# Two-layer hybrid decoder step: both halves of the next key pages turned at the head of a round, and gate halves dealt out to other rounds

## The reference

```python
gb, gc, hv, q, k, v, fl = jnp.split(h, splits, axis=-1)       # h = rmsnorm(x) @ w_in
yc, new_hist = causal_dwconv(gc * hv, hist, conv_w)           # 3 taps
y_a = gb * yc
...
s = jnp.einsum('bqhd,bkhd->bhqk', q, k) * (HEAD_DIM ** -0.5)  # 8 heads of 64
s = s + (cq[..., None] - ck[..., None, :])                    # sums of log forgets
p = jax.nn.softmax(jnp.where(k_pos <= q_pos, s, -inf), axis=-1)
out = jnp.einsum('bhqk,bkhd->bqhd', p, v)
...
k_all = jnp.concatenate([k_pool[page_table].reshape(bsz, p_len, h, d), k_new], axis=1)
```

## Time and profile before

| | us |
|---|---|
| median of 3 runs | 1504.37 |
| lowest, highest of them | 1501.26, 3993.2 |
| the profiled execution | 1502.65 |
| its span, first to last instruction | 1500.9 |
| TensorE busy in the span | 1409.4 (94%) |
| VectorE busy in the span | 721.5 (48%) |
| mean granted TensorE clock | 0.977 of full |

### The profile page before, as it was taken

The page is one execution under the profiler, slowest core; times in us unless marked ns, Lnnn a source line. Parts: engine busy times, 40 slices in busy tenths (PEclk is TensorE's granted clock), DMA queues, the critical chain, the costliest instruction groups (busy, mean ns, idle before and its releaser), DMA issues. The chain is left out here.

```text
span 1500.9 us, 34670 instructions
## 1 busy us (share of the span) xinstructions
PE 1409.4 (94%) x14005; PEld 1306.7 (87%) x14005; DVE 721.5 (48%) x1256; ACT 479.6 (32%) x706; POOL 594.9 (40%) x329
## 2 busy tenths in 40 slices
PE   7997888878799999999999999998999999999998
PEld 6895666666799999999999987875999999999998
DVE  5655678776444544203443366667455440044411
ACT  5474232233133222312223332116434422122221
POOL 2322222222233555444554454430445554455441
PEclk9998899998999999999999999998999999999999
DMA  5417679896632322333322446660423223323122
GB/s 180 127 52 237 230 262 319 302 336 200 213 88 67 97 84 73 92 102 91 92 63 62 134 125 163 153 167 2 124 62 93 84 67 101 113 82 87 52 80 74
DMA packets 246246, 192.56 MB, mean 128 GB/s; under 512 B 12129, under 2 KB 205106, under 8 KB 246058
## 3 DMA queue, kind: packets, MB, share of 16 engines
q1 hardware_dynamic: 244561, 188.31, 41.3%
q10 hardware_dynamic: 1181, 1.44, 0.4%
q0 software_dynamic: 400, 1.32, 0.3%
HBM read 173.03 MB, written 6.04 MB: 119 GB/s over the span
## 5 line engine op out<-in xcount | busy, mean ns | idle before, releaser
L683 POOL TENSOR_TENSOR w_l<-w_raw,w_h 128x1024 fp32r<-128x1024 f32 (+2 forms) x195 | 439.6, 2256 | 417.8 <-ACT w_h L830 397.0
L1804 PE MATMUL banks<-xa_h,w_h 128*128 128x272 f32 x1856 | 388.0, 290 | 4.4 <-DVE tmp L1627 3.3
L1804 PE MATMUL banks<-xa_h,w_l 128*128 128x272 f32 x1856 | 384.8, 289 | 0.0
L1804 PE MATMUL banks<-xa_l,w_h 128*128 128x272 f32 x1856 | 383.5, 288 | 0.0
L1804 PEld LDWEIGHTS banks<-xa_h,w_h 128*128 128x128 f32 x1856 | 293.2, 189 | 6.7 <-issue 5.4
L1804 PEld LDWEIGHTS banks<-xa_l,w_h 128*128 128x128 f32 x1856 | 292.4, 189 | 0.0
L1804 PEld LDWEIGHTS banks<-xa_h,w_l 128*128 128x128 f32 x1856 | 290.6, 189 | 0.0
L830 ACT ACTIVATE w_h<-w_raw 128x1024 fp32r<-128x1024 f32 (+2 forms) x193 | 185.1, 961 | 199.9 <-PE banks L1804 199.6
L1804 PE MATMUL banks<-h_h,w_h 128*128 128x272 f32 x928 | 192.7, 289 | 0.3 <-DVE x L1566 0.3
L1804 PE MATMUL banks<-h_h,w_l 128*128 128x272 f32 x928 | 192.3, 289 | 0.0
L1804 PE MATMUL banks<-h_l,w_h 128*128 128x272 f32 x928 | 191.6, 288 | 0.0
(11 more groups left out here) (302 smaller groups left out, 1682.3 us busy)
## 6 DMA issues: line engine op xcount, KB each, us to landing
w_raw<-in_w_up SPq DMA_DIRECT2D x88, 512.0 KB, 3.7
k_grp<-in_cache_k SPq DMA_DIRECT2D x128, 256.0 KB, 4.1
v_pg<-in_cache_v SPq DMA_DIRECT2D x120, 256.0 KB, 5.0
w_raw<-in_w_in SPq DMA_DIRECT2D x24, 512.0 KB, 6.0
w_raw<-in_w_down SPq DMA_DIRECT2D x32, 384.0 KB, 3.1
w_raw<-in_w_pw SPq DMA_DIRECT2D x24, 512.0 KB, 3.8
w_raw<-in_w_down SPq DMA_DIRECT2D x32, 320.0 KB, 3.0
w_raw<-in_w_out SPq DMA_DIRECT2D x8, 512.0 KB, 6.8
```

The source lines that it names most:

```text
L683: g.tensor_tensor(w_l[:, slot, 0:n], w_raw[:, slot, 0:n], w_h[:, slot, 0:n].bitcast(F32), ALU.subtract).then_inc(s_lo, 1)
L1804: ins = mm(out[:, half, 0:HT], w, v[:, half * HT:(half + 1) * HT], start=first and t == 0 and n == 0, stop=last and t == phase.tiles - 1 a ...
```

## The change

Two things change, the table of gate halves and the order of VectorE's program in a round.

```diff
 def gate_halves():
-    out = {0: ((0,), ()), 2: ((1,), (2,)), 3: ((3,), (4,)), 4: ((5,), (6,)), 16: ((18,), (19,)), 17: ((20,), (21,)),
+    out = {0: ((0,), ()), 2: ((1,), (2,)), 3: ((3,), (4,)), 4: ((5,), (6,)), 5: ((7,), ()), 6: ((8,), (9,)), 7: ((10,), ()), 8: ((11,), (12,)), 17: ((20,), (21,)),
            18: ((22,), (23,))}
-    for n in range(5, 16):
-        out[n] = ((n + 2,), ())
+    for n in range(9, 16):
+        out[n] = ((n + 4,), ())
...
                 if more:
                     key_turned(n + 1, 0)
+                    key_turned(n + 1, 1)
...
                 if n < PAIRS:
                     bias(2 * n)
                     bias(2 * n + 1)
+                    block_inverse(2 * n)
+                    block_inverse(2 * n + 1)
                 for q in halves_in(n):
                     half_scaled(q)
+                    if n < 17:
+                        gate_out(q)
+                if valued is not None and n >= 17:
+                    values(valued)
+                for q in halves_in(n) if n >= 17 else ():
                     gate_out(q)
-                if n < PAIRS:
-                    block_inverse(2 * n)
-                    block_inverse(2 * n + 1)
-                if more:
-                    key_turned(n + 1, 1)
                 if spread is not None:
                     total(spread)
...
-                if valued is not None:
+                if valued is not None and n < 17:
                     values(valued)
```

## The result

The changed kernel takes 1495.15 us in the median of its runs (1491.22 to 1501.35) against 1505.1 of the kernel before in the same session: a ratio of 0.9939, 95% interval 0.992 to 0.9959. It is faster by 10 us, 0.6%, where 25 were forecast. The profiled execution has a span of 1490.7 us against 1500.9. In the profile of after, lines beyond 1529 of the code are three higher than before (scores L1954, gate half L2073). Round 5 is scored at 192.58, round 15 at 343.96, and the output phase begins at 401.09.

A forecast was written before the change was run, and what follows sets the result against it. TensorE bounds the kernel, waiting in the attention stage for keys that VectorE turns late. Gains of 9 (start), 7 (middle) and 9 us (last part) make 25, for 1479.4 us; forecast range 1470 to 1490, overall 1465 to 1495.

The forecast's parts named there:

- the term of the gate halves: Rounds 6 and 8: one half more each on TensorE, 6.3 us added with nothing to hide them if rounds are tight.
- Rounds 5 to 14 by the order: Middle rounds: second turn at the head gives 13.5 us a round, ten rounds gaining 13 us on 147.8.
- the gate half waits for the logits: Middle rounds: a new TensorE wait for logits or `shift` in place of the key wait, about 1 us a round.
- TensorE's waits for keys went: TensorE's wait for turned keys, 21.0 us in ten waits up to round 15, should nearly vanish.
- VectorE waits openly for the exponential: Middle rounds: reciprocals wait for ScalarE's exponential, some 0.9 us a round, making VectorE alone 12.2.
- the landing chain of 12.8: Middle rounds: from the second key half's landing to scores two rounds on, 25.6 us, 12.8 a round, longest of three limits.
- Rounds 0 to 4: Start: the same waits for turned keys, 13.5 us, mostly go; 9 us gained, between 3 and 13.
- The last part: From round 15 on: 9 us gained, between 4 and 12, from the end and round 16.
- 4.6 for value pages: Round 16, halves gone: TensorE would wait about 5 us for round 17's value pages.
- 0.87 for `own`: The end: first wait for `own` goes, the second falls from 3.47 to about 0.9 us.
- 7.5 for the end: The end, by `values` earlier: 3.3 and 2.5 us of waits for `own` and 1.7 of a slow odd half gained.
- The rival at 1491: Late landings of the second key half hold VectorE's queue; middle gains 3, loses 6.3; 13 us in all; chance 0.2.

The follow-up runs named there:

- late_turn_even: old_table_tail_first with the second key half turned behind the logits in all even rounds from 6 to 14; 1470.57 us, ratio 0.9783.
- change_filled: The changed kernel with the small new-key matmuls of round 8 issued eleven times, 80 records more; 1489.06 us, ratio 0.9865.
- order_only: The changed kernel with the old table of gate halves: one in each of rounds 5 to 15, two in 16; 1476.48 us, ratio 0.9795.
- old_table_tail_first: order_only with the copy of the convolution's tail ahead of the last subtraction of a gate's low part; 1474.99 us, ratio 0.9787.
- before_filled: The kernel before with small new-key matmuls repeated, 24 records more in each of rounds 6 and 8; 1517.17 us, ratio 1.0089.
- table_only: The kernel before with only the new table of gate halves and the old order; 1515.68 us, ratio 1.0052.
- middle_as_before: The changed kernel with the second key half and reciprocals back behind the gate halves in rounds 5 to 14; 1498.25 us, ratio 0.9939.
- old_table_filled: order_only with small new-key matmuls of rounds 6 and 8 issued four times, 24 records more in each; 1489.24 us, ratio 0.987.

## Why the prediction was wrong

**The step that failed is the term of the gate halves**: "6.3 us added, nothing to hide them", for the two halves brought into rounds 6 and 8. With the new order, the table made rounds 5 to 14 longer by 14.2 us (137.2 to 151.4). The halves' 6.3 are right as far as they go; of the 7.9 beside them, 7.0 are pauses for TensorE's instruction supply (7.4 against 0.4), and the rest is slower matmuls. The halves also put 24 and then 48 matmul records ahead of everything later, and so move the block boundaries against the scores; in rounds 11 to 15 the boundary at which TensorE paused lay in or right behind the scores, where with the old table it fell on value pages 31 records or more behind them, and the packet of the block needed there started only when the scores were under way (in round 11, when they were over). Filler of as many records, without halves, does the same; filler that completes a block undoes it. The prediction costed what is issued by its duration alone, and had no term for it.

**Rounds 5 to 14 by the order** were right: 13.5 us a round forecast, 13.7 measured with the old table. The reasons were nearly right as well: the gate half waits for the logits (10.7 us in four waits, about 1 a round), TensorE's waits for keys went, and VectorE waits openly for the exponential, 6.5 us in ten rounds where 0.9 a round was taken. No wait of VectorE for a landing of keys stands in these rounds, and late_turn_even took 12.96 a round: the landing chain of 12.8 was not what held them in the order of the change.

**Rounds 0 to 4** gave 12.0 us, in the range of 3 to 13 but above the 9 taken. The new kernel's granted clock there is 0.95 instead of 0.85, and TensorE was busy 57.8 us instead of 62.4 with the same matmuls; what a wait costs afterwards had been left out of the value taken, and belonged in it.

**The last part** gave 2.6 instead of 9. This too is the supply for the most part: with the block completed by filler it takes 51.4 us instead of 59.7, 8.3 gained. Of the 5.7 us between the changed kernel and change_filled, 4.0 lie in round 15 from its scores to its gate half (11.6 us against 7.7): a pause of 1.83 us and slower matmuls around it. Another 1.5 lie from there to the pair of gate halves, at a granted clock of 0.77 against 0.91, and are not followed to a cause. The pair itself is slow in both (7.9 and 7.6 us instead of 6.3), behind the wait for pages, so that is not the supply's. A last part also differs by the clock alone: order_only took 54.8 us at 0.91, old_table_tail_first 50.3 at 1.00, with 0.6 us less to wait. The single steps came as forecast (4.6 for value pages, 0.87 for `own`), but for the wait of 1.93 for the tail's copy: the prediction moved `values` ahead without asking what the output phase needs of the operations now behind it. That is a mis-sized term, 7.5 for the end where 1.9 is given back.

The sum without the boundaries would have been 12.0 + (147.8 - 137.2 - 6.3) + 8.3 = 24.6 us, near the 25 on record. The sum on record was thus off by 7.9 us in the middle and 5.7 in the last part, with one cause for most of both. That the other terms meet the 25 so closely is partly luck: the start gave 3.0 more than was taken, and the middle without the boundaries 2.7 and the last part 0.7 less. The rival at 1491 came nearest to the number, for a reason that did not hold: landings did not hold VectorE. One bound of the prediction is also summed wrongly: with 28 us for the order and 6.3 for the halves, the middle part could have gained 22, not 19; nothing hangs on it.

What stays open: what sets off the request of a block, why only every second boundary paused, and how much the load of the DMA engines delays a packet. Of the 2.4 us from a packet's start to the next matmul, the packet itself takes about 0.9. None of this was tried. Of before_filled's 4.9 us beside its filler in rounds 5 to 14 (48 records, 2.9 us there), 3.5 are named pauses more than before; the rest is not followed to a cause.

## What to carry to other kernels

When short matmuls are as dense as here, count instructions as well as time: a stretch that uses up a block of instructions faster than one arrives will pause, and adding or moving work upstream shifts where that falls. In the trace it is "issue" in or behind a dense group, a packet of the instruction queue that starts inside or behind it, and pauses at fixed distances when the engine's records are counted (254 here); a packet inside the group is not enough, as round 15 of order_only shows. A filler of a known number of records tells within two runs whether it is that. And take a change of two parts apart before judging it: the order alone is worth 2%, and the table that came with it took most of that away.

## What the runs showed of the hardware

- TensorE's instructions come in packets of 16384 bytes, one for about 127 matmul records with their weight loads in the attention stage. In the pauses ending at 285.64, 333.34 and 348.35 the first matmul came 2.34 to 2.39 us after the packet's start, while 128 records of the scores take 2.67 us. In the changed kernel, the kernel before, table_only, middle_as_before, old_table_filled and before_filled the pauses of rounds 8 to 15 stand at the same record numbers within one, whole multiples of 254 apart, whatever work those records are. The Trainium skill (Runtime: NRT & Kernel Launch, Instruction fetch mechanics) has blocks of 256 instructions and calls the cost of crossing a boundary "mostly hidden". The size agrees nearly, if a record is a load and a multiply; the cost does not: 7.4 us of pauses in ten rounds, and up to 2.9 in one.
- The collision of VectorE with GpSimd can follow the order instead of the operation: the same copy took 0.18 us behind a subtraction and 1.77 ahead of it, and the subtraction 2.30 and 0.71, each stretch ending with GpSimd's split. Moving the stretched operation moved the stretch.
- Over rounds 5 to 14 the memory traffic rose with the speed of the rounds, from 300 GB/s to 320 and, in late_turn_even, 343 at a DMA share of 0.98. Round 13 of the kernel before reached 386 for 15 us, so 343 is not the most that they can give; whether they hold the next microsecond of these rounds, no run here tried.
